# A decoder block's expert stage: tokens moved to the output partitions, and the gathered expert rows summed on TensorE

## The reference

```python
experts = (e1 * N_KEYS + e2).reshape(t, PEER_HEADS * PEER_TOPK)   # 8 heads x 16 = 128 experts of 16384 for each token
gates = jax.nn.softmax(best, axis=-1).reshape(t, PEER_HEADS * PEER_TOPK)
...
u = expert_u[ic]
a = jax.nn.gelu(jnp.einsum('cd,ced->ce', xc, u), approximate=False) * gc
v = expert_v[ic]
return jnp.einsum('ce,ced->cd', a, v)
...
h = h + peer(...)
return rmsnorm(h, norm_final_g)      # y * rsqrt(mean(y*y) + EPS) * g
```

## Time and profile before

| | before |
|---|---|
| time, median of 2 runs | 1778.32 us (1778.12 to 1778.52) |
| span of the profiled execution | 1777.9 us |
| TensorE busy | 1709.2 us, 96% |
| VectorE busy | 1328.3 us, 75% |
| ScalarE busy | 793.7 us, 45% |
| GpSimd busy | 279.1 us, 16% |
| moved by DMA | 415.20 MB, mean 234 GB/s |

### The profile page before, as it was taken

One profiled execution on the slowest core, in us unless ns is written; L12 is line 12 of the kernel. 1 busy time (PEld: TensorE's weight loads), 2 busy tenths in 40 slices (PEclk: granted clock), 3 DMA queues, 4 the chain that ended last, 5 costly groups with the idle time before them and its releaser, 6 DMA issues.

```text
span 1777.9 us, 31302 instructions
## 1 busy us (share of the span) xinstructions
PE 1709.2 (96%) x9287; PEld 1599.5 (90%) x9287; DVE 1328.3 (75%) x2984; ACT 793.7 (45%) x1231; POOL 279.1 (16%) x267
## 2 busy tenths in 40 slices
PE   5999999998999999998999999999999999999996
PEld 4888788886789999998999999999999999999996
DVE  6555533334567999998988888778988888888886
ACT  4222533332333332325899999633333333333332
POOL 0000000000000000003222222343532222222220
PEclk9999999999999999999999999999999999999997
DMA  4233232223123445458999999999999999999992
GB/s 167 94 98 102 95 106 95 95 97 115 59 83 103 153 158 162 143 199 316 319 334 319 311 322 335 345 346 338 338 388 365 341 347 350 345 344 352 344 328 89
DMA packets 171524, 415.20 MB, mean 234 GB/s; under 512 B 14176, under 2 KB 90976, under 8 KB 169824
## 3 DMA queue, kind: packets, MB, share of 16 engines
q1 hardware_dynamic: 117344, 234.16, 38.8%
q0 software_dynamic: 36864, 134.23, 21.6%
q10 hardware_dynamic: 17280, 46.41, 6.6%
HBM read 366.25 MB, written 48.50 MB: 233 GB/s over the span
## 4 chain that ended last, share of the span: by engine, by line
PE 61%; DVE 12%; issue 10%; ACT 9%; DMA 5%; ACTq 2%; DVEq 1%; POOL 0%; POOLq 0%; SPq 0%
PE bank L812 10%; PE bank L813 10%; PE bank L814 10%; PE bank L680 10%; PE bank L682 10%; PE bank L681 10%; DMA rows<-u_rows,row_index 4%; ACT scratch L573 4%; ACT g_sb L586 3%; DVE e L1096 1%; DVE w_lo L845 1%; DVE found L1091 1%; ACT act_out L552 1%; PE bank L744 1%; DVE top_i L1034 1%
## 5 line engine op out<-in xcount | busy, mean ns | idle before, releaser
L845 DVE TENSOR_TENSOR w_lo<-w_raw,w_hi 128x1024 fp32r<-128x1024 f32 x348 | 425.4, 1223 | 223.0 <-ACT w_hi L451 222.9
L680 PE MATMUL bank<-xn_hi,w_hi 128*128 128x384 f32 (+1 forms) x1536 | 555.3, 362 | 16.1 <-DVE w_lo L845 9.7
L451 ACT ACTIVATE w_hi<-w_raw 128x1024 fp32r<-128x1024 f32 x348 | 367.3, 1056 | 455.6 <-PE bank L814 292.7
L682 PE MATMUL bank<-xn_hi,w_lo 128*128 128x384 f32 (+1 forms) x1536 | 546.8, 356 | 0.0
L681 PE MATMUL bank<-xn_lo,w_hi 128*128 128x384 f32 (+1 forms) x1536 | 546.7, 356 | 0.0
L812 PE MATMUL bank<-a_hi,w_hi 128*128 128x384 f32 x1024 | 344.9, 337 | 2.3 <-DVE a_lo L1227 2.2
L814 PE MATMUL bank<-a_hi,w_lo 128*128 128x384 f32 x1024 | 344.6, 337 | 0.0
L813 PE MATMUL bank<-a_lo,w_hi 128*128 128x384 f32 x1024 | 344.6, 337 | 0.0
L680 PEld LDWEIGHTS bank<-xn_hi,w_hi 128*128 128x128 f32 x1536 | 291.9, 190 | 47.3 <-issue 20.0
L423 POOL DMA_INDIRECT rows<-u_rows,row_index x128 | 139.8, 1092 | 1098.3 <-DVEq L1130 784.7
L682 PEld LDWEIGHTS bank<-xn_hi,w_lo 128*128 128x128 f32 x1536 | 291.7, 190 | 20.9
(11 more groups left out here) (172 smaller groups left out, 1481.8 us busy)
## 6 DMA issues: line engine op xcount, KB each, us to landing
w_raw<-u SPq DMA_DIRECT2D x128, 512.0 KB, 4.3
w_raw<-v SPq DMA_DIRECT2D x128, 512.0 KB, 6.2
g_dram<-g_sb ACTq DMA_DIRECT2D x12, 2048.0 KB, 10.7
g_in<-g_dram SPq DMA_DIRECT2D x32, 768.0 KB, 8.8
act_dram<-act_out ACTq DMA_DIRECT2D x108, 192.0 KB, 4.3
act_in<-act_dram SPq DMA_DIRECT2D x108, 192.0 KB, 6.0
w_raw<-w_in SPq DMA_DIRECT2D x32, 512.0 KB, 3.4
w_raw<-gate SPq DMA_DIRECT2D x32, 512.0 KB, 3.3
```

The lines of the kernel that those rows point to most:

```text
L451: act.activation(w_hi[:, slot, :], w_raw[:, slot, :], ACT.Copy).then_inc(hi_done, 1)
L680: pe.matmul(out, hi, act_hi[:, k, tokens], start=k == 0, stop=False)
L682: last = pe.matmul(out, lo, act_hi[:, k, tokens], start=False, stop=k == NB - 1)
L845: dve.tensor_tensor(w_lo[:, slot, :], w_raw[:, slot, :], w_hi[:, slot, :].bitcast(F32), ALU.subtract).then_inc(lo_done, 1)
```

## The change

**Orientation.** In the V stage the masked activations become the stationary operand (three blocks of 128 tokens), and the V rows the moving one, in halves of 512 channels: 3 token blocks x 3 products x 2 halves. The output has tokens on its partitions. Banks 0 to 5 hold the dense tokens, 6 and 7 the gathered ones (`V_BANK`).

**Gathered tokens.** The numbers of the chosen experts and the weighted dot products are transposed, so that a V gather brings the 128 rows of one token, one expert to a partition. Four such gathers make a group (32 groups). `v_rows` multiplies them on TensorE: for each of four tokens and two halves a product of 128 rows x 32 columns by 512 channels, into 32 PSUM partitions of its own. The 32 columns are those of `a_wide`, which GpSimd fills with zeros and VectorE fills on a diagonal, so that one column holds a token's 128 factors and 31 hold zeros. A group comes after every fourth tile, and at the start also after every second (eight groups in tile groups 3 to 6). GpSimd issues the four gathers of a group when the products of the group before are done. `accumulate`, `out_tok` and the `row_index` copies are gone, for the U rows too. The code of the V stage on TensorE and the gathers on GpSimd are written out without loops.

**Residual and norm.** `residual` adds `h_t` in PSUM by products with the identity (4 x 8). The last norm is done for each token on its partition: ScalarE squares from PSUM with a running sum, VectorE makes the factor and scales from PSUM. The last two tiles run token block by token block, so that the blocks finish one after the other. The gain comes as a [128, 1024] array, by one more load of 512 KB.

```diff
+FINAL_ORDER = (0, 1, 2, 3)
+V_BANK = (6, 0, 2, 4)
...
+        a_wide = xn_part("a_wide", [P, COL_TILES, TILE_TOKENS * (TILE_TOKENS + 1)])
+        a_diag = a_wide[:].rearrange("p j (m x) -> p j m x", x=TILE_TOKENS + 1)[:, :, :, 0]
...
-            def gather(table, r, slot):
-                pool.wait_ge(rows_used, r + 1)
-                pool.sem_inc(wait_carried, 1)
+            def gather(table, index, slot):
                 pool.indirect_dma_start(out=rows[:, slot, :], out_offset=None,
                                         in_=table.rearrange("a p d -> (a p) d"),
-                                        in_offset=bass.IndirectOffsetOnAxis(ap=row_index[:, slot:slot + 1], axis=0)
+                                        in_offset=bass.IndirectOffsetOnAxis(ap=index, axis=0)
                                         ).then_inc(rows_loaded[slot], 16)
-            for table, at in ((u_rows, 0), (v_d, PAIRS)):
-                with pool.Fori(0, PAIRS // ROW_SLOTS) as g:
-                    for slot in range(ROW_SLOTS):
-                        gather(table, ROW_SLOTS * g + (at + slot), slot)
+            pool.wait_ge(experts_ready, 1)
+            for r in range(PAIRS):
+                if r >= ROW_SLOTS:
+                    pool.wait_ge(rows_used, r - ROW_SLOTS + 1)
+                pool.sem_inc(wait_carried, 1)
+                gather(u_rows, expert[:, r:r + 1], r % ROW_SLOTS)
+            pool.wait_ge(experts_v, 1)
+            for t in range(GT):
+                if t < ROW_SLOTS:
+                    pool.wait_ge(rows_used, PAIRS - ROW_SLOTS + t + 1)
+                elif t % COL_TILES == 0:
+                    pool.wait_ge(v_rows_used, t // COL_TILES)
+                pool.sem_inc(wait_carried, 1)
+                token = t % COL_TILES * TILE_TOKENS + t // COL_TILES
+                gather(v_d, expert_v[:, token:token + 1], t % ROW_SLOTS)
+                if t == ROW_SLOTS - 1:
+                    pool.wait_ge(job_done, AT_V)
+                    pool.memset(a_wide[:], 0.0).then_inc(wide_zeroed, 1)
...
+            act.wait_ge(experts_turned, 1)
+            act.activation(expert_v[:], bank[7][:, 0:GT], ACT.Copy).then_inc(experts_v, 1)
+            act.wait_ge(experts_v, 1)
...
+            for n, c in enumerate(FINAL_ORDER):
+                if c == 0:
+                    act.wait_ge(v_rows_used, GT // COL_TILES)
+                else:
+                    act.wait_ge(acc_done, n)
+                for half in range(2):
+                    act.activation(scratch[:, half, :], bank[V_BANK[c] + half][:], ACT.Square,
+                                   accum_out=row_sum[:, c, half:half + 1]).then_inc(row_squared, 1)
+                act.wait_ge(row_var, n + 1)
+                act.activation(row_norm[:, 1, c:c + 1], row_norm[:, 0, c:c + 1], ACT.Sqrt).then_inc(row_root, 1)
...
+            pe.transpose(bank[7][:, 0:GT], expert_f[:], ident[:]).then_inc(experts_turned, 1)
...
-            def v_tile(g, b, first=False, final=False):
+            def v_ready(g, b):
                 pe.wait_ge(lo_done, SLOTS * g + (AT_V + b + 1))
                 pe.wait_ge(al_ready, SLOTS * g + (b + 1))
+            def v_chunk(c, b, first=False, final=False):
+                a_h, a_l = a_hi[:, b, (c - 1) * P:c * P], a_lo[:, b, (c - 1) * P:c * P]
+                for n, (stationary, moving) in enumerate(((a_h, w_hi), (a_h, w_lo), (a_l, w_hi))):
+                    for half in range(2):
+                        last = pe.matmul(bank[V_BANK[c] + half][:], stationary, moving[:, b, half * T:(half + 1) * T],
+                                         start=first and n == 0, stop=final and n == 2)
+                return last
+            def v_tile(g, b):
+                v_ready(g, b)
+                for c in range(1, CHUNKS):
+                    last = v_chunk(c, b)
+                last.then_inc(job_done, 1)
+            def residual(c, tokens, opens):
                 for j in range(NB):
-                    if first and j < SLOTS:
-                        pe.wait_ge(bank_free[j], USES_V + 1)
-                    hi, lo = k_block(w_hi, b, j), k_block(w_lo, b, j)
-                    out = bank[j][:, DENSE]
-                    pe.matmul(out, hi, a_hi[:, b, :], start=first, stop=False)
-                    pe.matmul(out, hi, a_lo[:, b, :], start=False, stop=False)
-                    last = pe.matmul(out, lo, a_hi[:, b, :], start=False, stop=final)
-                last.then_inc(job_done, 1)
+                    at = bank[V_BANK[c] + j // 4][:, j % 4 * P:(j % 4 + 1) * P]
+                    pe.matmul(at, tokens(j), ident[:], start=opens and j % 4 == 0, stop=False)
+            def v_rows(group):
+                for j in range(COL_TILES):
+                    pe.wait_ge(rows_loaded[j], 16 * group + (16 * (PAIRS // ROW_SLOTS + 1)))
+                for half in range(2):
+                    for j in range(COL_TILES):
+                        at = group_column(group, j)
+                        last = pe.matmul(bank[V_BANK[0] + half][j * TILE_TOKENS:(j + 1) * TILE_TOKENS, :], at,
+                                         rows[:, j, half * T:(half + 1) * T], start=False,
+                                         stop=group == GT // COL_TILES - 1)
+                last.then_inc(v_rows_used, 1)
+            def group_column(group, j):
+                return a_wide[:, j, group * TILE_TOKENS:(group + 1) * TILE_TOKENS]
             pe.wait_ge(g_copied, SLOTS + DT // TOKENS_PER_GROUP)
+            v_ready(0, 0)
             for b in range(SLOTS):
-                v_tile(0, b, first=b == 0)
-            with pe.Fori(1, U_STEPS - 1) as g:
+                pe.wait_ge(bank_free[b], USES_V + 1)
+            for c in range(1, CHUNKS):
+                last = v_chunk(c, 0, first=True)
+            last.then_inc(job_done, 1)
+            for c in range(1, CHUNKS):
+                residual(c, lambda j: h_t[:, j, c * P:(c + 1) * P], False)
+            for b in range(1, SLOTS):
+                v_tile(0, b)
+            for b in range(SLOTS):
+                v_tile(1, b)
+            v_tile(2, 0)
+            pe.wait_ge(dots_gated, 1)
+            pe.transpose(bank[V_BANK[0]][:, 0:GT], dots[:], ident[:]).then_inc(dots_turned, 1)
+            for b in range(1, SLOTS):
+                v_tile(2, b)
+            pe.wait_ge(wide_ready, 1)
+            residual(0, lambda j: h_t[:, j, 0:GT], True)
+            groups = 0
+            for g in range(3, U_STEPS - 1):
                 for b in range(SLOTS):
                     v_tile(g, b)
-            for b in range(SLOTS):
-                v_tile(U_STEPS - 1, b, final=b == SLOTS - 1)
-            pe.wait_ge(tok_done, 1)
-            for j in range(NB):
-                pe.transpose(bank[j][:, 0:GT], out_tok[:, j * P:(j + 1) * P], ident[:]).then_inc(acc_done, 1)
-            for j in range(NB // 2):
-                pe.wait_ge(added, 1 + j + 1)
-                sum_squares(0, squares[:, 2 * j, :], j)
-            spread_inverse(1, 3)
+                    if b == 3 or b == 1 and groups < GT // COL_TILES - (U_STEPS - 1 - g):
+                        v_rows(groups)
+                        groups += 1
+            assert groups == GT // COL_TILES, groups
+            for b in range(SLOTS // 2):
+                v_tile(U_STEPS - 1, b)
+            for b in range(SLOTS // 2, SLOTS):
+                v_ready(U_STEPS - 1, b)
+            for c in range(1, CHUNKS):
+                for b in range(SLOTS // 2, SLOTS):
+                    last = v_chunk(c, b, final=b == SLOTS - 1)
+                last.then_inc(acc_done, 1)
...
+            chain.did(dve.scalar_tensor_tensor(expert_f[:], flat(e2), float(KEYS), flat(e1), ALU.mult, ALU.add))
+            dve.scalar_tensor_tensor(expert[:], flat(e2), float(KEYS), flat(e1), ALU.mult, ALU.add
+                                     ).then_inc(experts_ready, 1)
             retrieve(HEADS - 1, 2, lambda b: u_split(TOPK_STEPS - 1, b))
...
-            def use_row(r, slot, times, use):
+            def dot(r, slot, times):
                 dve.wait_ge(rows_loaded[slot], 16 * times)
-                dve.tensor_copy(row_index[:, slot:slot + 1], expert[:, ds(r + ROW_SLOTS)])
-                use(r, slot).then_inc(rows_used, 1)
-            def dot(r, slot):
-                return dve.scalar_tensor_tensor(rows[:, slot, :], rows[:, slot, :], 1.0, x_tok[:], ALU.mult, ALU.mult,
-                                                accum_out=dots[:, ds(r)])
+                dve.scalar_tensor_tensor(rows[:, slot, :], rows[:, slot, :], 1.0, x_tok[:], ALU.mult, ALU.mult,
+                                         accum_out=dots[:, ds(r)]).then_inc(rows_used, 1)
...
-            def accumulate(r, slot):
-                return dve.scalar_tensor_tensor(out_tok[:], rows[:, slot, :], dots[:, ds(r - PAIRS)], out_tok[:],
-                                                ALU.mult, ALU.add)
-            def v_row(i, slot, times):
-                dve.wait_ge(rows_used, i + (ROW_SLOTS + PAIRS))
```

(24 more changed lines are left out.)

94 lines of the change are left out of this document (49 added, 45 removed).

## The result

| | before | after |
|---|---|---|
| time, median of 2 runs each | 1778.32 us | 1868.76 us (1864.12 to 1873.40) |
| ratio | | 1.048, 95% interval 1.037 to 1.060 |
| span of the profiled execution | 1777.9 us | 1871.6 us |

A forecast was written before the change was run, and what follows sets the result against it. TensorE, never idle late in the V stage, was taken as the bound. Dense -8, groups +130, switching +10.6, residual +7.4, waits +30, end -16 and U stage -3 sum to +151: 1929 us, range 1812 to 2010.

The forecast's parts named there:

- the group decides: V stage, gathered rows on TensorE: 1.7 us each makes the kernel measurably slower, 0.6 us is break-even.
- The gather waits: V stage, first eight groups, two tiles apart: TensorE waits 2.7 us, seven times; with half clock behind, +30 us.
- The end: After the last product: only the last block stays serial, 7.4 us in place of 23.2; -16 us.
- The residual: V stage, residual added on TensorE: 32 products of 128 columns, 64 records at 0.116 us; +7.4 us.
- The length of a float32 record of 512 columns: Gathered-row products on TensorE: one record at full clock taken as 0.45 us.
- The switching: Array running empty between whole and quarter width, twice a group: 64 x 0.165 us, +10.6 us (0 to 11).
- the length of the waits: Early groups: four gathers land 10.9 us (8.3 to 12.9) after release, against 8.2 us between groups; 2.7 us short.
- 9 steps: Gathered-row group on TensorE: two records run at any time, so 16 records take 9 x 0.45 = 4.05 us.
- two-abreast value: The likeliest case: a gathered-row group takes 4.05 us, +130 us over 32; total 1929 us, chance 0.40.
- four abreast: Rival for the gathered-row groups: all four column parts run together, 1.8 us a group; total 1857 us, chance 0.29.
- the dense products: V stage: 18 products at 0.2275 us a tile in place of 24 at 0.1727; -8 us over 128 tiles.
- the U stage: VectorE's 0.15 us copy and its loop registers go, twelve rows in a round of 50 us; -3 us (0 to -9).

The follow-up runs named there:

- the tile-outer order: Changed kernel with each group's eight products reordered: both halves for each column part, in place of all four parts for each half; 1867.54 us (one run).
- the kernel without products: Changed kernel with the gathered rows' products left out in groups 0 to 30, gathers and their waits kept; 1808.92 us, ratio 1.015.

## Why the prediction was right, and where it was wrong

**Right.** That TensorE is the bound and that taking work from VectorE buys nothing: VectorE fell by 36 points and no time came of it. That the group decides: 65.6 of 93.7 us. The gather waits, in place (seven, two tiles apart, none later), in length on average (2.8 for 2.7 us), and in their sum with the half clock: 27 us for 30. The end: 7.2 us for 7.4, -16 us. The residual. The length of a float32 record of 512 columns: 0.429 us, for 0.45. The switching: a group costs 0.33 us beyond its four steps, for 0.33 forecast; whether that is the array running empty, as the prediction has it, no run tells.

**Right in part by luck: the length of the waits.** The forecast took the median landing, 10.9 us from release to rows, and a half clock behind each wait. For the four long waits the last of the four gathers landed 7.3 to 8.6 us after its issue, so that the rows came 12.1 to 13.4 us after the first dense product behind the group before. For the three short ones it landed in 5.4 to 6.2 us, and the rows came after 10.4 to 10.9. Long and short alternate. Behind a long wait the two tiles take 0.9 us longer, part of it at half clock, and the DMA engines have less to do: from the first issue to the group their share is 0.78 to 0.79 for the three short waits and 0.97 to 0.99 for the four long ones. That this share sets how soon the gathers land is argued, not shown. The errors offset in the sum, and "2 to 3 us each" holds for none of the seven.

**Wrong, the step that failed:** "If products start in order, the first record of the next product starts only with the second of this one ... the 16 records take 9 steps". They take four. The group was forecast at 4.05 + 0.33 us and measured at 2.05, 75 us less over 32. The rows of before could not show it, as the prediction said; but the two-abreast value rested on an inference from order alone, between bounds a factor of four apart. The kernel whose groups use one part gives 6.98 us, the tile-outer order leaves the four parts abreast, and with that both halves of the step are answered: the parts run together, and order across parts does not bind them. Had I taken four abreast, the same working gives 1857 us, 12 under the result. So the time lies in the range because the range took in that rival, and not because the likeliest case came.

**Mis-sized: the dense products**, -8 forecast (the two figures beside it, 4.095 and 4.145 us, give -6.4), +5 measured. The 0.2275 us came from rows of the query stage, whose operands lie low; the V stage's activations, now stationary, lie high, and there the pace is 0.2333. The prediction named a change of this pace as what would make it wrong, and looked for it in the stationary block's repetition; the runs put it in the block's place. The pace of before was misread a little too (0.1727 for 0.1733 us), which works the other way, by 2 us.

**Wrong sign, small: the U stage**, -3 forecast, +4.5 measured. The copy that went was held to be pure load on VectorE; ScalarE, at 96%, kept its time, and GpSimd's issues grew longer. No run shows the gain that was forecast; what makes the loss, and how much of it is scatter, stays open.

## What to carry to other kernels

When work moves to the engine that is never idle, all that counts is its price there; relief elsewhere is worth nothing until that engine waits for it. For narrow products, give each 32-column part its own share: four parts brought 3.8 times here, in both orders tried, even with float32's two records, but a product with one useful column in 32 is still dear beside one VectorE instruction that nobody waits for. A pace read from rows holds for operands in those places: when 512-column products set the time, read the pace of every stage separately, and try both operands low in the partition (below byte 114,816 here).

## What the runs showed of the hardware

- Records in the four column parts start 6 to 7 ns apart and run together; 16 float32 records of 512 columns take 1.85 us in four parts and 6.98 us in one, with a step of 0.429 us in both.
- Records of one column part follow one another, but records of another part that stand later in TensorE's list do not wait for them: the group takes 1.87 us with four records of each part in a row, where list order would give 5.6.
- Going from 128 to 32 columns and back cost 0.33 us in all. The Trainium skill, "TensorEngine Tiling (Array Packing)", Key Properties, says that a change of tiling mode drains TensorE; the 0.33 us here agree with a short drain, and no run takes it away. Behind a wait, when TensorE had stood, the second dense product also came late (0.31 us after the first, in the kernel without products at 1298.60 us), much as the 0.34 behind a group.
- Products of 512 columns start every 0.2333 us when their stationary block lies at byte 139,936 of a partition or above, and every 0.2267 us when it lies at 92,288. With the moving operand it is much the same (0.234 us from byte 124,448 on); there the contents differ as well. Where between 114,816 and 124,448 it sets in, by what mechanism, and why 384-column products show nothing of the kind (0.1733 us with `a_hi` moving at 139,808, and as much in the U stage with `xn_hi` moving below 114,816), stays open.
- GpSimd issues an indirect gather in 0.93 to 1.2 us mostly, and in about 2 us in 2 to 14 of 128 cases, more often where VectorE's long instructions stand back to back.
- How long TensorE waited does not tell by itself whether the clock falls: in the changed kernel waits of 3.4 to 4.7 us had half clock behind them and one of 3.1 us had not, and in the kernel before one of 2.2 us had.
